# Neighbourhood attention block: another order of the modulation weight steps, and the projection pieces spread over ten ticks

## The reference, cut to what matters

```python
mod = c_act @ w_ada[i] + b_ada[i]                 # 1024 -> 6 * 1024
sh_a, sc_a, g_a, sh_f, sc_f, g_f = jnp.split(mod, 6, axis=-1)
h = _modulate(x, sh_a, sc_a)
qkv = (h @ w_qkv)                                 # 1024 -> 3 * 1024
s = q . k over a window of 8 rows x 16 columns + bias
p = softmax(s);  o = p . v
x = x + g_a * (o @ w_o)
```

## Time and profile before

| | |
|---|---|
| median of 3 runs | 1784.76 us (1782.65 to 1786.32) |
| the profiled execution, its own time | 1784.59 us |
| its span, first to last instruction | 1782.8 us |
| mean granted TensorE clock | 0.898 |
| neighbourhood block, first transposes to those of the feed-forward | 477.70 to 654.34 us |
| PE busy over the span | 1511.9 us (85%) |
| DVE, ACT busy over the span | 1239.6 us (70%), 856.9 us (48%) |

### The profile page before, as it was taken

One profiled execution on the slowest core, in us unless ns is written; L12 is line 12 of the kernel. 1 busy time (PEld: TensorE's weight loads), 2 busy tenths in 40 slices (PEclk: granted clock), 3 DMA queues, 4 the chain that ended last, 5 costly groups with the idle time before them and its releaser, 6 DMA issues.

```text
span 1782.8 us, 21828 instructions
## 1 busy us (share of the span) xinstructions
PE 1511.9 (85%) x7686; PEld 1228.7 (69%) x7686; DVE 1239.6 (70%) x1592; ACT 856.9 (48%) x1195; POOL 45.9 (3%) x55
## 2 busy tenths in 40 slices
PE   2799879999699768999758996499999999999993
PEld 1787668777588558989545665477777777777772
DVE  7777548674565557887654223488888888888885
ACT  0544444354444333433233112276777776776772
POOL 0000000000100000000000000000000000000001
PEclk9989899898899789999867558599999999999997
DMA  9755327353276327877431003097797797797792
GB/s 401 277 203 212 119 80 279 149 195 112 83 283 224 119 80 270 302 273 301 170 113 48 1 1 134 26 365 305 313 418 310 314 418 309 312 417 313 310 402 83
DMA packets 61528, 403.08 MB, mean 226 GB/s; under 512 B 6534, under 2 KB 9734, under 8 KB 15116
## 3 DMA queue, kind: packets, MB, share of 16 engines
q1 hardware_dynamic: 52416, 379.45, 54.6%
q10 hardware_dynamic: 7020, 15.30, 2.4%
q0 software_dynamic: 2016, 7.34, 1.1%
HBM read 393.14 MB, written 8.91 MB: 226 GB/s over the span
## 4 chain that ended last, share of the span: by engine, by line
PE 53%; DVE 24%; ACT 7%; issue 7%; DMA 6%; POOL 1%; SPq 1%; DVEq 0%; ACTq 0%; POOLq 0%
DVE w_lo L1978 13%; PE PS L781 12%; PE PS L782 12%; PE PS L783 12%; DMA raw<-in_ws 6%; PE PS L880 4%; ACT w_hi L1464 3%; ACT xg L1591 2%; DVE acc L1995 1%; PE PS L901 1%; PE PS L1011 1%; PE PS L890 1%; PE PS L991 1%; PE PS L868 1%; PE PS L1256 1%
## 5 line engine op out<-in xcount | busy, mean ns | idle before, releaser
L1978 DVE TENSOR_TENSOR w_lo<-raw,w_hi 128x2048 fp32r<-128x2048 f32 x287 | 657.9, 2292 | 162.9 <-ACT w_hi L1464 135.9
L1464 ACT ACTIVATE w_hi<-raw 128x2048 fp32r<-128x2048 f32 x287 | 548.6, 1920 | 252.0 <-PE PS L783 204.4
L781 PE MATMUL PS<-w_hi,h_hi 128*128 128x512 f32 (+2 forms) x812 | 338.1, 416 | 36.8 <-DVE w_lo L1978 14.4
L782 PE MATMUL PS<-w_lo,h_hi 128*128 128x512 f32 (+2 forms) x812 | 320.4, 395 | 0.0
L783 PE MATMUL PS<-w_hi,h_lo 128*128 128x512 f32 (+2 forms) x812 | 319.7, 394 | 0.0
L781 PE MATMUL PS<-h_hi,w_hi 128*128 128x256 f32 x776 | 231.7, 299 | 20.8 <-DVE h_lo L2023 11.6
L782 PE MATMUL PS<-h_lo,w_hi 128*128 128x256 f32 x776 | 224.2, 289 | 0.0
L783 PE MATMUL PS<-h_hi,w_lo 128*128 128x256 f32 x776 | 224.0, 289 | 0.0
L781 PEld LDWEIGHTS PS<-w_hi,h_hi 128*128 128x128 f32 x812 | 157.0, 193 | 86.3 <-DVE w_lo L1978 29.1
L1995 DVE SCALAR_TENSOR_TENSOR acc<-raw,cs,acc 128x512 f32<-128x512 f32 x252 | 189.4, 752 | 8.9
L783 PEld LDWEIGHTS PS<-w_hi,h_lo 128*128 128x128 f32 x812 | 156.9, 193 | 33.3
(11 more groups left out here) (308 smaller groups left out, 1544.5 us busy)
## 6 DMA issues: line engine op xcount, KB each, us to landing
raw<-in_ws SPq DMA_DIRECT2D x359, 1024.0 KB, 6.1
y_rows<-ysb ACTq DMA_DIRECT2D x10, 512.0 KB, 8.5
rp<-in_rp ACTq DMA_DIRECT2D x8, 384.0 KB, 4.7
ckb<-in_ck ACTq DMA_DIRECT2D x2, 1024.0 KB, 4.8
y_rows<-ones ACTq DMA_DIRECT2D x3, 512.0 KB, 9.6
x<-in_x SPq DMA_DIRECT2D x1, 1024.0 KB, 11.3
gpost<-in_gpost ACTq DMA_DIRECT2D x2, 512.0 KB, 5.3
x_rows<-xn_f ACTq DMA_DIRECT2D x2, 512.0 KB, 2.8
```

The lines of the kernel that those rows point to most:

```text
L781: t.matmul(out, lhs[0], rhs[0], start=start, stop=False, skip_group_check=True)
L782: t.matmul(out, lhs[0], rhs[1], start=False, stop=False, skip_group_check=True)
L1464: a.activation(wh[:, SPL_AT[e.phase][i], :], raw[:, r, :], ACT.Copy).then_inc(*e.inc("hi"))
L1978: v.tensor_tensor(wl[:, s, :], raw[:, r, :], wh[:, s, :].bitcast(F32), ALU.subtract).then_inc(*e.inc("raw_used"))
```

## The change

The order of steps becomes w0 w1 w2 a0a w3 a0b w4 a1a w5 a1b w6 a2a w7 a2b w8 a3a w9 a3b w10 a4a w11 a4b w12 a5a w13 a5b w14 w15: one modulation half behind each w step from w2 on. The pieces per tick are 3 2 2 3 2 2 2 2 2 2 in ticks 0 to 9 in place of 3 in each of ticks 0 to 7, and two pieces are done ahead, between `ada(0)` and the wait for the banks that stands before `scores(0)`. `NA_RAW` goes; DVE takes ada steps as they come up on the way to the next w step, and a5b in tick 10. PE's wait for the last slot's banks moves from tick 9 to tick 10, with the pieces. The wait for `h` 6 in tick 13 now stands before `ada(5)` and not behind it.

```diff
-NA_FILL = [(1, 2)] * 8 + [(0, 0)] * (NA_TICKS - 8)
+NA_AHEAD = 2
+NA_FILL = [(1, 2), (1, 1), (1, 1), (1, 2), (1, 1), (1, 1)] + [(1, 1)] * 4 + [(0, 0)] * (NA_TICKS - 10)
-NA_RAW = {8: 23, 9: 24, 10: 25, 11: 26, 12: 26}
 def na_steps_before(tick):
-    return 6 + sum(a + b for a, b in NA_FILL[:tick]) // 4
+    return 6 + (NA_AHEAD + sum(a + b for a, b in NA_FILL[:tick])) // 4
 def na_steps():
-    halves = dict(zip((2, 4, 5, 7, 8, 9, 10, 11), (x for j in range(4) for x in ada_steps(j))))
+    halves = dict(zip(range(2, 14), (x for j in range(6) for x in ada_steps(j))))
     out = []
-    for n in range(14):
+    for n in range(16):
         out.append(("w", n))
         if n in halves:
             out.append(halves[n])
-    return out + ada_steps(4) + ada_steps(5) + [("w", 14), ("w", 15)]
+    return out
...
                 ada(0)
-                for b in LAY_BANK[0:6]:
+                fill, out = projections(), out_first()
+                for _ in range(NA_AHEAD):
+                    next(fill)
+                for b in LAY_BANK[1:6]:
                     pe.wait_ge(*e.at(f"bank{b}", 1))
                 scores(0)
-                fill, out = projections(), out_first()
...
-                    if i == 9:
+                    if i == 10:
                         for q in (10, 11):
                             pe.wait_ge(*e.at(f"bank{LAY_BANK[q]}", lay_uses(q)))
...
+                    if i == 13:
+                        pe.wait_ge(*e.at("h", 6))
                     if i in NA_ADA:
                         ada(NA_ADA[i])
...
-                    if i == 13:
-                        pe.wait_ge(*e.at("h", 6))
...
-                    if i < 8:
-                        split_to(min(na_steps_before(i) + SPL, 14))
-                    elif i < 13:
-                        raw_to(NA_RAW[i])
-                    else:
-                        split_to(15)
+                    split_to(min(na_steps_before(i) + SPL, 14) if i < 13 else 15)
+                    if i == 10:
+                        raw_to(26)
```

## The result

The changed kernel took 1787.82 us (median of 20 runs, 1782.5 to 1790.8), the kernel before 1784.18 us (20 runs, 1779.74 to 1788.46). The ratio is 1.0021, with a 95% interval of 1.0011 to 1.003: 3.6 us slower by the medians. The forecast was 11.5 us faster. The profiled execution took 1787.83 us, with a span of 1786.0 us.

A forecast was written before the change was run, and what follows sets the result against it. PE was taken to bound the block, by its waits and the half clock after them. Gains of 16.6 and 4.6 us less losses of 7.8 and 1.9 made 11.5 off 1784.6: 1773.1 us, chance 0.72, range 1768.5 to 1781.

The forecast's parts named there:

- The waits that go: Before ada(4) and near slot 5: waits of 6.9 and 3.4 us and 6.3 of half clock go, together 16.6.
- Two pieces ahead: Before scores(0): two pieces fill the wait, 2.9 us go, and 1.7 of half clock behind it, together 4.6.
- The start: Before turn_probs(0): a2a and a2b delay logits(0); a new wait of 5.7 us and 2.1 of half clock, 7.8 lost.
- Ticks 1 to 9: DVE's heavy ticks take 6.7 us against PE's 5.0, but 3 us of slack hide it: no loss.
- slot 4's copies: Tick 6 has one piece less to cover ACT's copies of 2.39 us: 0.5 us lost.
- Tick 8: lo_part comes first and waits for ACT; exponentials ready at 12.3 us, asked for at 14.6: no loss.
- Slot 5's copies: Before scores(11): ACT's two copies, 1.08 us, no longer covered; with the release on both sides 1.4 us lost.
- The clock: New half clock only behind the start's new wait: 2.1 us lost, bounded by 0 and 4.9.
- B: Rival: half clock after the start's new wait costs 4.9 us in place of 2.1; 1775.9 us, chance 0.12.
- C: Rival: DVE bounds the ticks, five heavy ticks cost PE 8.5 us in all; 1781.6 us, chance 0.10.
- D: Rival: thinner ticks stay at half clock, 10 us each; slower, 1793 us with four such ticks; chance 0.06.

The follow-up runs named there:

- e1: The changed kernel with hi_part(1) and lo_part(1) in tick 9, behind slot 5's copies, in place of tick 8: 1774.72 us, ratio 0.9943.
- e7: The changed kernel with pieces 3 2 2 3 2 3 2 3 2 in nine ticks, the last in tick 8: 1780.52 us, ratio 0.9979.
- e8: The changed kernel with hi_part of half 0 waiting for 11 used split steps in place of 12: 1780.0 us, ratio 0.9981.
- e2: The changed kernel with a5a ahead of lo_part(1) in DVE's tick 8, in place of behind it: 1785.48 us in one run.
- e5: e1 with a2a and a2b no longer ahead of w8, and a4b behind w13 in tick 8: 1774.73 us, ratio 0.994.
- e9: e5 with a4b ahead of w13, in tick 7, in place of behind it in tick 8: 1771.67 us, ratio 0.9932.
- e10: e9 with hi_part(1) and lo_part(1) left in tick 8, hi_part(1) waiting for 11 used steps: 1773.75 us, ratio 0.9944.
- e12: e8 with w13 in tick 9 and a5a staying in tick 8: 1775.38 us, ratio 0.9951.
- e11: e9 with w13 rounded and subtracted in tick 9 in place of tick 8: 1768.61 us, ratio 0.9911.
- e3: The kernel before with the new order of steps alone: three pieces in each of ticks 0 to 7, none ahead: 1781.27 us, ratio 0.9977.
- e4: The changed kernel's pieces alone, two ahead and the rest over ten ticks, with order of steps and NA_RAW as before: 1780.74 us, ratio 0.9975.
- e6: e5 with hi_part(1) and lo_part(1) still in tick 8: 1779.29 us in one run.

## Why the prediction was wrong

- **The waits that go: right.** 6.9 and 3.4 us, and the half clock from 587 to 607, are gone. e1 shows their worth, since it keeps all of the change: 9.9 us faster than before.
- **Two pieces ahead: right.** 2.9 forecast, 3.7 - 0.7 = 3.0 measured, and no half clock behind `scores(0)`.
- **The start: right in kind and size.** The wait before `turn_probs(0)` was forecast at 5.7 and is 5.6, from ACT's exponentials, with `logits(0)` 6 us later. The half clock behind it cost 2.7, not 2.1.
- **Ticks 1 to 9: right up to tick 7.** PE never waits there, and slot 4's copies cost nothing, where I had 0.5.
- **Tick 8: the step that failed.** The prediction said of it: "In tick 8 `lo_part` comes first and waits for ACT: exponentials ready at 12.3, asked for at 14.6". It took ACT's `hi_part` to be ready after `copy_pt(8)`. The wait of `hi_part` for twelve used split steps, visible in the code and free in the trace of before (the last piece had then long ended), was not carried over to the new place of the last piece. e1 (moved), e7 (one tick less) and e8 (eleven steps) each show it; e8 puts it at 5.9 us of wait.
- **Slot 5's copies: the second step that failed.** "ACT's two copies take 1.08 us, with the release on both sides 1.4" left out what stands ahead of them in ACT's queue: exp(10), and through it logits(10), w13 and a5a on DVE. I had worked out that these exponentials come 12.3 us after the start of tick 8, and set that against `turn_probs(10)` (14.6) alone. PE asks for slot 5 much sooner: in the changed kernel tick 8 begins at 578.7 and PE stands from 588.4, 9.7 us on. 12.3, a copy of 0.6 and slot 5's 1.1 less 9.7 are 4.3 us, and e8, in which only this row is left, measured 4.1. The forecast had 1.4 for it.
- **The clock.** The forecast had half clock behind the wait at the start alone. In the profiled run the 10.0 us brought 6.2 more. How much follows a wait is not settled by its length: in e2 some 2 us followed 8.2 (last section). Forecast 9.7 lost in all, measured 24.5; gained 21.2 forecast, 21.3 measured.
- **The rivals.** B (the start costs more) was 0.6 of its 2.8. C (DVE bounds the ticks) is not what happened in this kernel, since e1 leaves the load and takes the wait. But in e5, e9 and e10, once the start is mended, the series of DVE and ACT within a tick does hold PE up, and in e8 a part of C is true of one tick: e12 takes w13 alone out of DVE's tick 8, and 2.3 of the 4.1 us go. D had the sign right, by another mechanism: the ticks 1 to 9 kept 1.00 throughout. Whether the change is slower by more than the 0.2% that D asks for is open, since the interval, 1.0011 to 1.003, has 1.002 inside. The Trainium skill, "TensorE: Matmul & The Clock Gate", section "HAM oscillation — how this bites in real kernels", tells of bursts of matmuls that start at half clock because each stands behind a long wait. The trace agrees for the two long waits of the changed kernel (0.54 over the 5.96 us behind the first, 0.51 over the 12.60 us behind the second); the thin ticks had no such waits and ran at 1.00.

What stays open: why the part of the kernel that no edit touches differs by up to 6.9 us between the profiles, where by these profiles e11's missing 1.6 to 4.6 us lie, and why nearly the same wait before nearly the same work is followed by some 4 us of work at half clock in one kernel and by 12 in another (last section).

## What to carry to other kernels

When work moves later on one engine, look up every wait whose count it raises, those that never showed in the trace included: a semaphore that was free before ("all uses of this buffer") can be the one that binds, as here, and the instruction that waits holds its whole queue (5.81 us of ACT's and 8.32 us of DVE's). For each wait of the bottleneck, write down the whole queue ahead of the releasing instruction and date the slowest, not the releasing instruction's own length. Price a new wait, too, with the half clock that follows it: here it came behind each wait of 3.4 us or more of the block's ticks, in all profiles, and cost 1.5 to 6.3 us on top. And when kernels differ by a few us, compare the part that was edited by the trace as well as the whole time.

## What the runs showed of the hardware

Ticks with two pieces in place of three kept the clock at 1.00. After waits of 1.2 and 1.8 us (e11, e1) it stayed there as well. After 4.1 us in e8 it fell, and the next 12.10 us of work ran at 0.53; after 5.4 us in e9 the next 12.30 at 0.51; after 10.0 us 12.60 at 0.51. e8's stages (stretch, length, PE, clock, DMA share, GB/s):

```profile
588.20:592.30 4.10, 0.01 (x1) 0.73 0.97 396
592.30:604.40 12.10, 12.10 (x33) 0.53 0.32 121
```

But the bill behind a wait does not follow from its length. In e5 the wait was 5.7 us, in e9 5.4, and PE then had the same products to do: `scores(11)`, `ada(4)`, `values(8)`, `turn_probs(10)`. `scores(11)` with the wait before it, and `values(8)`, in e5 and then in e9:

```profile
587.30 2.05 PE L1257 MATMUL PS<-nakz,naq 128*128 128x512 f32 x2 [5.66 <-ACT nav L1845]
592.24 1.10 PE L1276 MATMUL PS<-nav,ptn 128*128 128x64 f32 x8
```

```profile
583.31 2.05 PE L1257 MATMUL PS<-nakz,naq 128*128 128x512 f32 x2 [5.36 <-ACT nav L1845]
588.99 1.97 PE L1276 MATMUL PS<-nav,ptn 128*128 128x64 f32 x8
```

`scores(11)` takes 2.05 us in both; `values(8)` takes 1.10 in e5, at full clock again, and 1.97 in e9, still at half. All profiles side by side, in us: the wait of tick 10, the work at half clock behind it, the block from `xn_n` to `xn_f` on DVE, and the rest of the span, which no edit touches.

| run | wait | at half clock | block | rest |
|---|---|---|---|---|
| before | 6.9 | 9.9 | 176.6 | 1606.2 |
| changed | 10.0 | 12.4 | 179.6 | 1606.4 |
| e1 | 1.8 | none | 165.9 | 1604.4 |
| e2 | 8.2 | 3.9 | 175.4 | 1608.3 |
| e3 | none | none | 171.3 | 1608.2 |
| e4 | 11.5 | 12.4 | 173.0 | 1607.4 |
| e5 | 5.7 | 4.2 | 163.5 | 1609.9 |
| e6 | 11.4 | 12.2 | 173.0 | 1604.4 |
| e7 | 4.9 | 4.6 | 172.2 | 1606.7 |
| e8 | 4.1 | 11.4 | 173.2 | 1604.7 |
| e9 | 5.4 | 11.9 | 167.1 | 1603.0 |
| e10 | 5.8 | 3.7 | 165.3 | 1607.2 |
| e11 | 1.2 | none | 158.0 | 1608.4 |
| e12 | 1.8 | none | 165.5 | 1608.0 |

At a granted clock of 0.50, 4 us of such work cost 2 us and 12 cost 6. In e2, e7 and e10 another 3.4 us of work ran at half clock later in the block (e10: 615.8 to 619.2), just behind a wait of 1.5 us that the other kernels have as well and that was followed by none there. Each kernel has one trace, so whether these amounts belong to the kernel or to the one execution is not shown. Behind the 5.58 us at the start the level came back within 5.96 us of work (clock 0.54). The last column differs by up to 6.9 us, nearly twice the 3.6 us by which the change was slower. For the change itself this does no harm, since the rest is alike before and after (1606.2 and 1606.4) and the block grew by 3.0; between the runs e1 to e12 it can hide or feign a few us.
